# A two-block transformer kernel: memory rows first in the front, w_ada over 53 pieces, and the two attention halves overlapped step by step

## The reference, cut to what matters

```
shift, scale, gate = split(silu(c) @ w_ada[l] + b_ada[l])        # for c and for c_ctx; w_ada[l] is 2048 x 6144
h, hc = rms_norm(x)*(1+scale)+shift, rms_norm(ctx)*(1+scale_c)+shift_c
p, pc = h @ w_in[l], hc @ w_in[l]                                # 6144 columns: pooled, gates, q, k, v
q, k  = rope(rms_norm(q)), rope(rms_norm(k))                     # 8 heads of two halves of 64
a     = softmax(q1 k1') - lam * softmax(q2 k2');  o = a @ v      # x: 512 keys, ctx: its own 256
x     = x + gate * (concat(pool(p)*silu(.), rms_norm(o)*silu(.)) @ w_out[l])
# second block, later: mem_n = rms_norm(mem);  mem_n @ w_k,  mem_n @ w_v       (256 rows of memory)
```

## Time and profile before

| | us |
|---|---|
| median of 3 runs (lowest, highest) | 3529.5 (3526.95, 3530.09) |
| the profiled execution, its own time | 3530.72 |
| its span, first to last instruction | 3529.0 |
| PE busy in it | 3460.7 (98%) |
| DVE, ACT, POOL busy | 2043.5, 1650.3, 218.6 |
| mean granted TensorE clock | 0.996 |

### The profile page before, as it was taken

How to read it: one execution, slowest core, us unless ns; L and a number is a source line. 1 busy time by engine, 2 the same in 40 slices (tenths; PEclk the granted TensorE clock), 3 DMA queues, 4 the chain that set the end, 5 groups by cost and what they waited for, 6 DMA issues and landing times.

```text
span 3529.0 us, 44614 instructions
## 1 busy us (share of the span) xinstructions
PE 3460.7 (98%) x16522; PEld 2810.5 (80%) x16522; DVE 2043.5 (58%) x2475; ACT 1650.3 (47%) x2157; POOL 218.6 (6%) x409
## 2 busy tenths in 40 slices
PE   7999999999999999999999999999999999999998
PEld 5777777778888877788888888888888888888887
DVE  4666545543477656556457775566644566666544
ACT  5442134443345235545446554444454466666443
POOL 1010010101000010000010000000000000000000
PEclk9999999999999999999999999999999999999999
DMA  9989942424566854556676767665654555555654
GB/s 361 358 262 388 341 142 90 155 78 163 201 201 222 281 171 149 199 202 194 218 250 209 225 229 230 214 236 188 209 170 148 188 186 185 184 185 184 202 192 160
DMA packets 331246, 736.77 MB, mean 209 GB/s; under 512 B 26359, under 2 KB 26961, under 8 KB 327872
## 3 DMA queue, kind: packets, MB, share of 16 engines
q1 hardware_dynamic: 300224, 627.12, 53.7%
q0 software_dynamic: 30704, 106.24, 8.5%
q10 hardware_dynamic: 144, 1.05, 0.1%
HBM read 689.10 MB, written 45.21 MB: 208 GB/s over the span
## 4 chain that ended last, share of the span: by engine, by line
PE 92%; DVE 4%; ACT 2%; DMA 1%; issue 1%; POOL 0%; ACTq 0%; SPq 0%; DVEq 0%; POOLq 0%
PE psum L702 28%; PE psum L704 28%; PE psum L703 28%; PE psum L539 1%; DVE w_lo L602 1%; PE psum L1212 1%; PE psum L1228 1%; ACT w_hi L594 1%; PE psum L1270 1%; PE psum L1255 1%; PE psum L2388 1%; PE psum L1220 1%; PE psum L2030 0%; PE psum L766 0%; PE psum L2198 0%
## 5 line engine op out<-in xcount | busy, mean ns | idle before, releaser
L602 DVE TENSOR_TENSOR w_lo<-w_raw,w_hi 128x1024 fp32r<-128x1024 f32 x997 | 1218.6, 1224 | 1236.6 <-ACT w_hi L594 1234.2
L594 ACT ACTIVATE w_hi<-w_raw 128x1024 fp32r<-128x1024 f32 x997 | 1052.9, 1059 | 1328.7 <-PE psum L704 1276.0
L702 PE MATMUL psum<-w_hi,a_hi 128*128 128x512 f32 x3072 | 1220.1, 397 | 4.4 <-DVE a_lo L1312 1.9
L704 PE MATMUL psum<-w_hi,a_lo 128*128 128x512 f32 x3072 | 1200.5, 391 | 0.0
L703 PE MATMUL psum<-w_lo,a_hi 128*128 128x512 f32 x3072 | 1199.3, 390 | 0.0
L702 PEld LDWEIGHTS psum<-w_hi,a_hi 128*128 128x128 f32 x3072 | 579.1, 188 | 131.2 <-issue 9.9
L704 PEld LDWEIGHTS psum<-w_hi,a_lo 128*128 128x128 f32 x3072 | 578.1, 188 | 122.4
L703 PEld LDWEIGHTS psum<-w_lo,a_hi 128*128 128x128 f32 x3072 | 579.2, 189 | 115.2
L702 PE MATMUL psum<-w_hi,f_hi 128*128 128x512 f32 x704 | 276.3, 393 | 0.0
L704 PE MATMUL psum<-w_hi,f_lo 128*128 128x512 f32 x704 | 274.6, 390 | 0.0
L703 PE MATMUL psum<-w_lo,f_hi 128*128 128x512 f32 x704 | 274.2, 390 | 0.0
(11 more groups left out here) (390 smaller groups left out, 2842.6 us busy)
## 6 DMA issues: line engine op xcount, KB each, us to landing
w_raw<-w_in SPq DMA_DIRECT2D x416, 512.0 KB, 4.2
ada_raw<-w_ada SPq DMA_DIRECT2D x192, 512.0 KB, 7.0
w_raw<-ffn_w_up SPq DMA_DIRECT2D x176, 512.0 KB, 3.4
w_raw<-w_out SPq DMA_DIRECT2D x96, 512.0 KB, 4.6
w_raw<-ffn_w_down SPq DMA_DIRECT2D x88, 512.0 KB, 4.0
p<-stage POOLq DMA_DIRECT2D x152, 256.0 KB, 4.5
w_raw<-xa_w_k SPq DMA_DIRECT2D x32, 512.0 KB, 8.5
w_raw<-xa_w_v SPq DMA_DIRECT2D x32, 512.0 KB, 6.5
```

The lines of the kernel that those rows point to most:

```text
L594: nc.scalar.activation(w_hi[:, slot], raw_of(k), ACT.Copy).then_inc(hi_ready, 1)
L602: nc.vector.tensor_tensor(w_lo[:, slot], raw_of(k), w_hi[:, slot].bitcast(F32), ALU.subtract).then_inc(lo_ready, 1)
L702: nc.tensor.matmul(acc, g.hi[:, tt, kt, :], w_hi[:, slot, kk, :], start=first, stop=False)
L704: mm = nc.tensor.matmul(acc, g.lo[:, tt, kt, :], w_hi[:, slot, kk, :], start=False, stop=last)
```

## The change

- Front: mem_sb is loaded by SP, first of all. The turns go in the order n = 2*g + k, the order in which pieces need them (piece j needs group g = j // 2 of both halves). PE makes four turns and multiplies one w_ada block, then the pieces begin; the other four turns are steps of early_pe behind pieces 0 to 3.
- w_ada: one block ahead instead of six; groups at steps 1, 4, ..., 52, over front and cover; unit 3's additions at 9 to 46; unit 8's and 9's additions in lanes0 from step 6 on, 32 blocks in 22 steps, not in 28 from step 0. SP asks for the first blocks behind pieces 0 to 3. The modulation is read five steps later (MOD_STEP 11).
- Attention: `staggered` starts the second half when the first has made its last unit's scores (step 2+7+units), without empty steps, and the closing stage likewise. The rate is 1.0 in layer 0, and 1.0, 0.6875, 1.0 in layer 1. Loads of the second half's rows move to fit; the squares of a closing use half of e_sb instead of rt.
- Pooling: the second of two matmuls for a column tile takes only columns 120 to 255 of poolA, the others being zero.

```diff
-        ADA_LEAD = 6
+        ADA_LEAD = 1
-        LEAD_HOMES, LEAD_STEPS = (198, 64, 68, 72, 76, 198), (-4, -4, -3, -2, -1, -1)
+        LEAD_HOMES, LEAD_STEPS = (198,), (-1,)
...
-            (plan["front"], range(ADA_LEAD, KT * 3), (64, 68, 72, 76, 198), range(2, 48, 3), 4,
-             range(KT * 3, KT * 4), (56, 60), [4 + n * 36 // 15 for n in range(16)], {44: 3}),
+            (mem_kv, range(ADA_LEAD, KT * 3), (64, 68, 72, 76, 198), range(1, 53, 3), 4,
+             range(KT * 3, KT * 4), (56, 60), [9 + n * 37 // 15 for n in range(16)], {49: 3}),
...
-             range(KT * 8, KT * 10), (160, 164, 198), [n * 28 // 32 for n in range(32)], {19: 8, 29: 9}),
+             range(KT * 8, KT * 10), (160, 164, 198), [6 + n * 22 // 32 for n in range(32)], {19: 8, 29: 9}),
...
-            for k in range(XT):
-                pool.dma_start(mem_sb[:, k, :], t["mem_2"][0, k * P:(k + 1) * P, :]).then_inc(mem_loaded, 16)
...
+            for _ in range(gr["idle"]):
+                yield
             slots, turned = slots_of(gr)
             for n in range(len(slots) + 1):
+                if hg and n == 1:
+                    load_qk(pool, gr, hg, 2)
                 if turned.get(n) == 0:
                     load_qk(pool, gr, hg, 3)
+                    if hg:
+                        values()
                 yield
             for s in range(len(gr["units"]) + 2):
-                if following and s == len(gr["units"]) - 2:
+                if following and s == len(gr["units"]) - 4:
...
-                act.wait_ge(qk_done, gr["m0"] + 4)
-                nc.scalar.activation(rt[:], o_tok[:, 2 * c:2 * c + 2, :].rearrange("p t c -> p (t c)"), ACT.Square).then_inc(on_sq, 1)
+                act.wait_ge(a_ready, gr["n0"] + len(units))
+                nc.scalar.activation(o_squares, o_tok[:, 2 * c:2 * c + 2, :].rearrange("p t c -> p (t c)"), ACT.Square).then_inc(on_sq, 1)
...
-                for m in range(XT):
-                    mm = nc.tensor.matmul(psum[:, b, 256 * (cc % 2):256 * (cc % 2) + 256], pv[:, m, cc * P:(cc + 1) * P],
-                                          poolA[:, cc // 2, m, :], start=m == 0, stop=m == XT - 1)
+                for m, first in ((0, 0), (1, P - 8)):
+                    mm = nc.tensor.matmul(psum[:, b, 256 * (cc % 2) + first:256 * (cc % 2) + 256], pv[:, m, cc * P:(cc + 1) * P],
+                                          poolA[:, cc // 2, m, first:], start=m == 0, stop=m == XT - 1)
...
+        def staggered(l, first, second, closing):
+
+            units = len(attn[l][0]["units"])
+            second_at = attn[l][0]["idle"] + 7 + units
+            going = [(0, first), (second_at, second), (second_at + 7 + units + 2, closing)]
+            step = 0
+            while going:
+                for part in list(going):
+                    if part[0] <= step:
+                        try:
+                            next(part[1])
+                        except StopIteration:
+                            going.remove(part)
+                step += 1
+                if going:
+                    yield
...
-        ATTN_RATE = [1.125, [1.25] * 2 + [0.75] * 4 + [1.0] * 2]
+        ATTN_RATE = [1.0, [1.0] * 2 + [0.6875] * 4 + [1.0] * 2]
...
+        LEAD = 4
...
+        def lead_turn(pe, n):
+            g, k = divmod(n, XT)
+            if g == 0:
+                pe.wait_ge(fin_stored if k else mem_loaded, 16)
+            if n >= 3:
+
+                pe.wait_ge(turn_lo, n - 2)
...
         def lead_pe(pe):
+            pe.sem_inc(turn_src, XT)
+            for n in range(LEAD):
+                lead_turn(pe, n)
             ada_pe(pe, 0)
-            ada_pe(pe, 1)
-            pe.wait_ge(mem_loaded, 32)
...
         def early_pe(pe):
+            for n in range(LEAD, 4 * XT):
+                lead_turn(pe, n)
+                if n % 2:
+
+                    pe.wait_ge(turn_lo, n - 1)
+                yield
+            yield
+            pe.wait_ge(turn_lo, 4 * XT)
+            yield
             cols_pe(pe)
...
-        MOD_STEP = 6
+        MOD_STEP = 11
...
         def _(sp):
-            for a in range(ADA_FIRST):
-                load_ada(sp, a)
+            for k in range(XT):
+                sp.dma_start(mem_sb[:, k, :], t["mem_2"][0, k * P:(k + 1) * P, :]).then_inc(fin_stored if k else mem_loaded, 16)
             for g in order:
                 stream_in(sp, g)
...
             lead_pe(pe)
-            pe.wait_ge(turn_lo, 4 * XT)
+            pe.wait_ge(turn_lo, XT)
```

More of the change, by code:

```diff
@@ L369, in build_program @@
         ada_count, total_count, landings = {}, {}, [0] * 6
-        used = added = groups = 0
+        used = added = 0
+        groups = 1
         def place(a, home, step):
@@ L1039, in group_act @@
         def group_act(act, gr):
-            yield
-            yield
+            for _ in range(gr["idle"]):
+                yield
             slots, turned = slots_of(gr)
@@ L1081, in group_act @@
                         act.wait_ge(a_ready, n - 1)
+                    if s == 1 and gr["c0"]:
+                        act.wait_ge(on_ssq, gr["c0"])
                     sm = 112 + 8 * (n % 2)
@@ new lines, in first_pool @@
+        def first_pool(pool, l):
+            first = plan["lanes0"][2] if l == 0 else plan["lanes1"][1]
+            rows_ready = [(ada_used, max(total_count[u][0] for u in (7, 9, 11)[:2 + l]))] + stored_by(first)
+            following = (attn[l][1], stored_by(plan[f"beside{l}"][1 - l]))
+            for n, _ in enumerate(group_pool(pool, attn[l][0], l, 0, rows_ready, [], following)):
+                if n == 1:
+                    gate_rows_pool(pool, l)
+                if n == 11:
+                    gate_keep_pool(pool, l)
+                yield
@@ L2629, in attention_act, with first_dve @@
+        def first_dve(dve, link, l):
+            for n, _ in enumerate(group_dve(dve, link, attn[l][0])):
+                if n == 10:
+                    gate_rows_dve(dve, link, l)
+                yield
+        def attention_pool(pool, l):
+            second = group_pool(pool, attn[l][1], l, 1, [], stored_by(plan[f"beside{l}"][l]), None)
+            return staggered(l, first_pool(pool, l), second, close_pool(pool, l))
         def attention_act(act, l):
-            for gr in attn[l]:
-                yield from group_act(act, gr)
@@ new lines, in lead_turn @@
+        def lead_turn(pe, n):
+            g, k = divmod(n, XT)
+            if g == 0:
+                pe.wait_ge(fin_stored if k else mem_loaded, 16)
+            if n >= 3:
+                pe.wait_ge(turn_lo, n - 2)
+            for b in range(4):
+                kt = 4 * g + b
+                mm = nc.tensor.transpose(psum[:, 5 + n % 3, b * P:(b + 1) * P], mem_sb[:, k, kt * P:(kt + 1) * P], ident[:])
+            mm.then_inc(turn_T, 1)
+        def lead_act(act):
+            lead_hi(act, 0)
+            lead_hi(act, 1)
+            prologue_hi(act, 0)
+            prologue_hi(act, 1)
+            lead_hi(act, 2)
+            lead_hi(act, 3)
+            prologue_hi(act, 2)
@@ L2757, in early_dve @@
         def early_dve(dve, link):
+            for n in range(LEAD, 4 * XT):
+                lead_lo(dve, n)
+                yield
+            dve.sem_inc(turn_tmp, 4 * XT)
+            yield
+            yield
             yield
@@ L2828, in opening_pool @@
         def opening_pool(pool):
+            for _ in range(MOD_STEP - 6):
+                yield
             mod_pool(pool, 0)
```

113 lines of the change are left out of this document (42 added, 71 removed).

## The result

The changed kernel takes 3504.4 us (median of 4 runs, 3501.2 to 3505.1) against 3529.3 (4 runs, 3526.95 to 3530.09): ratio 0.9929, 95% interval 0.9912 to 0.9946. It is 24.9 us faster where 36.4 were forecast, and the time lies just above the range. The profiled execution is the fastest of the four, 3501.2 us; that of before, 3530.7, was slower than all four of its timed runs, so the two traces are 29.4 us apart.

The account below looks back on a forecast made before the run. TensorE was taken as the bound, busy 3460.7 of 3529.0 us. Savings 19.0+4.9+10+2.5 = 36.4 us took the profiled 3530.7 to 3494.3, or 3493.0 since the median run was 1.2 faster; range 3485 to 3504.

Parts of the forecast that it names:

- beside0 (19.0 and 1.6): Attention stage beside0: staggering the halves leaves no piece with two steps of one half, 19.0 us less; its narrower pooling 1.6.
- The 1.8 that I took for the clock of the piece at 511.36: In beside0, the piece behind two turns, at granted clock 0.77: 8.53 less 6.69 us, counted within the 19.0.
- Pooling (4.9): Three poolings: 16 matmuls each narrowed to 136 columns, 1.6 us less per pooling, 4.9 in all, bounds 0 and 5.
- Start (14.9): Kernel start: first product at 15.9 us instead of 30.79, 14.9 earlier; bounds for it 15.3 and 18.
- So the pace is there, with little to spare: Front's DMA: 74.3 MB needed before piece 53 in 203.8 us, 365 GB/s; mean was 352, later window 406.
- I take 10 from the front: Front: start 14.9 us earlier, less 1.8, 2.4 and 0.6 of moved work, leaves 10.1 at piece 53; 10 taken.
- Rival 1: Front stays DMA-bound at 352 GB/s: piece 53 at 214.5, 3 us earlier instead of 10; time 3500; chance 0.15.
- The clock: Start of the front: first pieces again pay for running at 1.2 GHz, 0 to 1.4 us more or less.
- beside1 (2.5, and 1.6 of pooling): Attention stage beside1: four-tile pieces gain 2.8 us, two-tile part keeps its waits, 0.3 lost; bounds -3 and +6; pooling 1.6 more.
- rival 2: Closings and norms of two halves queue; PE waits once in beside0 (5 us), twice 2.5 in beside1: 3503; chance 0.10.
- Rivals 3 and 4: Every unit step waits, 3541 at 1 us each, chance 0.02; beside0 unchanged and front DMA-bound, above 3522, chance 0.03.
- The signs: Wrong if w_raw or ada_raw lands late in first 100 us, PE waits at second half's first turns, or single steps cost more.

Follow-up runs that it names:

- p_front: Kernel before with only the front, w_ada steps and moved modulation of the change; attention and pooling as before: 3526.8 us, ratio 0.9990.
- p_pool: Kernel before with only the narrower second pooling matmul: 3526.7 us, ratio 0.9992.
- p_whole: The whole change again, timed beside its parts, against the kernel before: 3504.4 us, ratio 0.9928.
- lead8: Whole change, but all eight turns of the memory rows stand ahead of the first product again: 3502.3 us, ratio 0.9916.
- x_sp: Whole change, but rows of x and first half of ctx loaded by SP's queue between weights, not POOL's: 3502.3 us, ratio 0.9923.
- x_sp_seam1_g5: Whole change plus x and ctx rows on SP's queue, two empty steps between layer 1's halves, w_ada's second group at piece 5: 3498.1 us, ratio 0.9908.
- wide0: x_sp_seam1_g5 with the first of three poolings back at its old width of 256 columns: 3498.8 us, ratio 0.9912.

## Why the prediction missed

By the medians of the parts, the 36.4 us forecast became 2.7 of 10 for the front, 17.4 of 21.5 for attention and 2.7 of 4.9 for the pooling.

- **beside0 (19.0 and 1.6): the mechanism right, the size 3 to 5 us too high.** The traces differ by 20.3 of 20.6 us, but that agreement is partly luck: the sum was made from, and compared with, an execution of before that was slow in this stage. The traces of p_front and p_pool, whose attention is that of before, take 457.2 and (with the narrow pooling) 455.5 us where before's takes 460.4, because its pieces 8, 40, 47 and 48 ran longer at half clock. The 1.8 that I took for the clock of the piece at 511.36 is 1.3 too much by them. Against 457.2, beside0 is 17.1 us shorter in the changed kernel's trace and 15.5 in p_whole's, with pooling.
- **Pooling (4.9): price nearly right, one place lost.** Each is 1.60 us shorter by its matmuls and 1.50 from product to product, and 5.5 us long (the 5.1 in the prediction's last paragraph doesn't follow from its own sum). But the clock falls to half at the start of wout0 in every trace whose first pooling is narrow, and takes 1.55 us back. Of three times 1.50 that leaves 3.0; p_pool measured 2.7.
- **Start (14.9): right.** First product at 16.01. Four turns and the constants took what was worked out.
- **Front: here the prediction failed**, at "So the pace is there, with little to spare" and "I take 10 from the front". At piece 53 the gain is 4.5 us in the changed kernel's trace (212.90 against 217.35), 1.4 in p_whole's, 0.9 in p_front's; by the medians p_front is worth 2.7. Beyond the 4.8 us of moved work, front, cover and lanes0 together lose 3.7 in the changed kernel's trace. The waits, 4.3 in sum, cover it: for w_ada +3.4, for xn_T +1.5 (6.0 against 4.5), for xn +0.6, for mem_lo +0.5, less the 1.7 us that PE waited at the start of lanes0 before. In p_whole's trace they lose 6.5 and in p_front's 6.6, mostly because the clock falls to half in the front as well (a mean of 0.97 in p_front's). I had divided all bytes up to piece 53 by all the time. That mean holds (358 GB/s over front and start), but the shortage sits in the first 40 us, where blocks have the least lead and POOL's queue takes 64% of the bytes from 20 to 32 us. Rival 1 named the right resource and nearly the time (214.5 for piece 53, between these traces' 212.9 and 216.5), with the wrong shape: not a low mean over 200 us but a local one. lead8 shows that the early start meets missing data: 7.6 us of it are worth 0.9 or less at piece 9. How the loss divides between the shared queue, the order of the transfers and the buffers is open: x_sp takes 2.4 us off the waits for w_ada and x_sp_seam1_g5 another 1.2, with no time gain beyond the intervals.
- **The clock.** The first pieces paid the half clock again in the changed kernel's trace, as forecast (p_whole's first product took 0.47 us, at full clock). More of it came later in other executions: the granted clock is 0.5 at about 41 and again at 116 us in p_whole's trace and never in the changed kernel's front, which is 2.9 us shorter. That is the larger part of the 3.5 us between the two; 1.6 more lie in beside0, and beside1 gives 1.1 back. So the trace shown above is a lucky one, 3 us under the median, and its 29.4 us overstate the gain.
- **beside1 (2.5, and 1.6 of pooling): 2.6 in the traces for the sum of 4.1, sizes wrong.** The four-tile part gave 9.1 and not 2.8; the two-tile part took 6.5, or 8.0 without its shorter pooling, and not 0.3. That the stage's two-tile pieces "keep their waits" failed: the closing of the first half in front of the second's norms, which I added to DVE without a price, lengthens PE's longest wait there from 2.3 to 4.7 us. That is rival 2's seam, once instead of twice, and within its price of 5 us. The seam in beside0 cost 1.9 us, 3.5 with the half clock behind it.
- **Rivals 3 and 4** are out: single steps cost in the changed kernel what they cost before, in every piece compared, and beside0 gained.
- **The signs.** Two of the three named signs of being wrong came: w_raw and ada_raw land late in the first 100 us, and PE waits at the second half's first turns. The third, dearer single steps, did not.

The Trainium skill (DMA: Bandwidth & Descriptors, "Where 436 GB/s comes from") puts the HBM limit of one core at about 358 GB/s. The window above moved 4.92 MB in 12 us, 410 GB/s, so that limit does not show here. By that figure the front would have given 6 us, an estimate; it gave 4.5 or less, but not by a limit on the total.

## What to carry to other kernels

A start that is moved forward is worth only as much as the data of its first pieces allows: go through the first ten pieces one by one, with what each needs, when it was asked for and who else is on the wire, and don't divide all bytes by all time. A cheap test that tells this at once is to delay the start by design and see whether the tenth piece moves. Sum a forecast from more than one trace of before, where single pieces can carry a half clock that the next execution doesn't have. Where two series are overlapped, price the engine with two jobs at the seam against the products of one piece there, and check it behind the shortest pieces, not the long ones.

## What the runs showed of the hardware

- Two DMA queues don't share evenly by bytes: with 8 KB packets on POOL's queue and smaller ones on SP's, POOL's got 3.15 MB and SP's 1.76 in 12 us; with 2 KB packets 2.59 and 2.07, at a total 5% lower. The Trainium skill (DMA: Bandwidth & Descriptors, "Queues, rings and completion order") says that a DMA engine takes turns between its queues and finishes a whole packet of one before it goes to the next. The direction agrees with these rows (longer ones, more bytes); the size doesn't follow from the packets that the profile counts: ones a quarter as long took only a sixth off POOL's bytes.
- One wait of 1.93 us at the same place leaves the clock at 2.4 GHz in four traces and halves it in ten. The ten have the narrow first pooling, some 70 us earlier, the four have not, and wide0 turned it back. So a wait of this length can cost 1.93 us, or that plus some 1.5, and a saving can come back as half clock elsewhere. The moment of the stage doesn't decide: the narrow ones reach it between 889.8 and 914.1 us, the wide ones at 893.8, 902.2, 912.7 and 918.7. By what path work 70 us earlier acts on the clock is open.
